# First weight splits, bias strips and the output projection's first weights, each at another place in a two-layer kernel

## The reference, cut to what matters

```python
def hybrid_layer(x, norm1_w, w_in, w_a2, b_a, gla_norm_w, w_out, norm2_w, w_ff1, w_ff2, rel_bias):
    h = rmsnorm(x, norm1_w)
    proj = h @ w_in
    aq, ak, av, bq, bk, bv, br, ba, cq, ck, cv = jnp.split(proj, ..., axis=-1)
    y_a = dilated_attention(heads(aq, 6), heads(ak, 6), heads(av, 6), bias_a)   # bias by distance
    y_b = gla(...)                                                              # gated linear attention
    y_c = moba_attention(heads(cq, 6), heads(ck, 6), heads(cv, 6), bias_c)      # bias by distance
    mix = jnp.concatenate([y_a, y_b, y_c], axis=-1)
    x = x + mix @ w_out
    h2 = rmsnorm(x, norm2_w)
    return x + jnp.square(jax.nn.relu(h2 @ w_ff1)) @ w_ff2
```

## Time and profile before

| what | us |
|---|---|
| median of three executions | 1555.93 (1555.65 to 1557.7) |
| profiled execution, its own time | 1553.91 |
| span of that execution, first to last instruction | 1552.1 |
| TensorE busy in the span | 1495.3 (96%) |
| ScalarE, VectorE, GpSimd busy | 577.2, 799.1, 657.9 |
| mean granted TensorE clock, of full speed | 0.987 |

### The profile page before, as it was taken

One profiled execution on the slowest core, in us unless ns is written; L12 is line 12 of the kernel. 1 busy time (PEld: TensorE's weight loads), 2 busy tenths in 40 slices (PEclk: granted clock), 3 DMA queues, 4 the chain that ended last, 5 costly groups with the idle time before them and its releaser, 6 DMA issues.

```text
span 1552.1 us, 21717 instructions
## 1 busy us (share of the span) xinstructions
PE 1495.3 (96%) x7323; PEld 1190.3 (77%) x7323; DVE 799.1 (51%) x1258; ACT 577.2 (37%) x948; POOL 657.9 (42%) x314
## 2 busy tenths in 40 slices
PE   8999999999999999999999899998999999999997
PEld 6778667788888888877768687665887888888886
DVE  4382384552443435864994505564556565654121
ACT  5412572431323223323972325553223232222222
POOL 4433455445444444434334345452443444444442
PEclk9999999999999999999999999999999999999998
DMA  5534202354555555423333234110332333333332
GB/s 154 157 88 117 82 28 69 124 178 153 174 158 158 168 163 168 129 68 94 91 81 90 60 103 75 35 41 14 95 95 68 99 100 99 95 95 91 98 94 85
DMA packets 285177, 160.27 MB, mean 103 GB/s; under 512 B 44930, under 2 KB 272770, under 8 KB 285114
## 3 DMA queue, kind: packets, MB, share of 16 engines
q1 hardware_dynamic: 285114, 159.46, 35.7%
HBM read 156.78 MB, written 5.80 MB: 105 GB/s over the span
## 4 chain that ended last, share of the span: by engine, by line
PE 48%; issue 34%; POOL 11%; DVE 3%; ACT 3%; DMA 1%; POOLq 0%; ACTq 0%; SPq 0%; DVEq 0%
PE ps L1981 13%; PE ps L1983 13%; PE ps L1982 13%; POOL WL L654 11%; PE ps L2464 2%; PE ps L2217 1%; PE ps L2475 1%; PE ps L2488 1%; PE ps L2277 1%; PE ps L2291 1%; PE ps L2334 1%; ACT WH L768 0%; DVE UL L1662 0%; ACT LP L1204 0%; DVE actL L1607 0%
## 5 line engine op out<-in xcount | busy, mean ns | idle before, releaser
L654 POOL TENSOR_TENSOR WL<-Wraw,WH 128x1024 fp32r<-128x1024 f32 (+2 forms) x239 | 573.2, 2399 | 810.3 <-ACT WH L768 810.3
L768 ACT ACTIVATE WH<-Wraw 128x1024 fp32r<-128x1024 f32 (+2 forms) x239 | 246.2, 1031 | 738.4 <-PE ps L1983 727.4
L1981 PE MATMUL ps<-actH,WH 128*128 128x512 f32 x1256 | 501.5, 399 | 15.7 <-POOL WL L654 8.8
L1983 PE MATMUL ps<-actH,WL 128*128 128x512 f32 x1256 | 490.5, 391 | 0.0
L1982 PE MATMUL ps<-actL,WH 128*128 128x512 f32 x1256 | 490.3, 390 | 0.0
L1981 PEld LDWEIGHTS ps<-actH,WH 128*128 128x128 f32 x1256 | 236.4, 188 | 82.2 <-issue 14.2
L1983 PEld LDWEIGHTS ps<-actH,WL 128*128 128x128 f32 x1256 | 236.5, 188 | 50.4
L1982 PEld LDWEIGHTS ps<-actL,WH 128*128 128x128 f32 x1256 | 236.6, 188 | 49.5 <-issue 2.9
L1981 PE MATMUL ps<-UH,WH 128*128 128x512 f32 x576 | 228.7, 397 | 7.8 <-DVE T L1835 4.1
L1983 PE MATMUL ps<-UH,WL 128*128 128x512 f32 x576 | 225.9, 392 | 0.0
L1982 PE MATMUL ps<-UL,WH 128*128 128x512 f32 x576 | 225.8, 392 | 0.0
(11 more groups left out here) (275 smaller groups left out, 1484.9 us busy)
## 6 DMA issues: line engine op xcount, KB each, us to landing
Wraw<-in_w_ff SPq DMA_DIRECT2D x64, 512.0 KB, 4.1
Wraw<-in_w_in SPq DMA_DIRECT2D x56, 512.0 KB, 3.9
wada<-in_w_ada SPq DMA_DIRECT2D x64, 384.0 KB, 4.5
Wraw<-in_w_up SPq DMA_DIRECT2D x44, 512.0 KB, 3.8
Wraw<-in_w_down SPq DMA_DIRECT2D x16, 448.0 KB, 3.7
Wraw<-in_w_proj_rnn SPq DMA_DIRECT2D x16, 320.0 KB, 3.1
Wraw<-in_w_proj_mla SPq DMA_DIRECT2D x8, 512.0 KB, 3.8
Wraw<-in_w_out SPq DMA_DIRECT2D x8, 512.0 KB, 3.8
```

What stands on the lines that cost most here:

```text
L654: nc.gpsimd.tensor_tensor(WL[slot][:, 0:kts, :], Wraw[slot][:, 0:kts, :], WH[slot][:, 0:kts, :].bitcast(F32), ALU.subtract).then_inc(s_lo, 1)
L768: A(WH[slot][:, 0:kts, :], Wraw[slot][:, 0:kts, :], ACT.Copy).then_inc(s_hi, 1)
L1981: MM(o, wh, ah, start=first, stop=False)
L1983: return MM(o, wl, ah, start=False, stop=last)
```

## The change

1. In the head ScalarE first loads its table with an activation on one column of `ones`, then splits weight block 0, then makes high parts 0 and 1, splits block 1, and goes on; the squares of x's first half are cut into two and two, and those of its last two quarters stand behind the last high parts. `x_squared` counts one more.
2. The strips' DMA leaves SyncE's queue and is issued by ScalarE, behind the `Silu` that ends the decay chain and ahead of the split of block 2 of `gQK`. The wait for the table stood there already.
3. The first two blocks of `gOut` are split behind `a_step(2)` and `a_step(3)`, on ScalarE and on GpSimd.
4. VectorE does `a_step(6)` ahead of `gla_low`; TensorE's first pair of `gOut` goes through the tiles as 0 to 4, 6, 7, 5 where it was 6, 7, 0 to 5.
5. The turning of the linear attention's result comes behind tile 6 of block 13, where it was behind tile 4.
6. The second norm's last sum comes at step 7, where it was at step 6.

```diff
@@ SyncE
             for c in range(4 * PAIRS // 2):
-                if c == 2:
-                    sp.wait_ge(S("tab_stored"), 16)
-                    sp.dma_start(strip_dram, bass.AP(tab_dram.tensor, P - 1, [[TAB, 2 * PAIRS], [-1, P], [1, SEQ]])
-                                 ).then_inc(S("strips_stored"), 16)
                 qk_load(c, c // 4, c % 4)
@@ GpSimd
                 for i in range(TB):
                     a_normalize(p, i)
-            lows(gOut, 2, 1)
+                if p in (2, 3):
+                    low(gOut.n0 + p - 2, gOut.slot(p - 2))
@@ ScalarE, head
+            act.wait_ge(S("ones_set"), 1)
+            A(T[5][:, 0:1], ones[:, 0:1], ACT.Copy).then_inc(S("x_squared"), 1)
+            highs(gB, 1, 1)
             act.wait_ge(S("vecs_turned"), 1)
             x_high(0)
             x_high(1)
-            highs(gB, 1, 1)
+            highs(gB, 1, 1, first=1)
             x_high(2)
             x_high(3)
             act.wait_ge(S("x_loaded0"), 16)
             act.wait_ge(S("x_loaded1"), 16)
-            x_squares(0, 2, 0, 2 * part)
-            highs(gB, 1, 1, first=1)
+            x_squares(1, 2, 0, 2 * part, range(2))
             x_high(4)
             x_high(5)
-            act.wait_ge(S("x_loaded2"), 16)
-            x_squares(TB, 3, 2 * part, 3 * part)
+            x_squares(3, 2, 0, 2 * part, range(2, TB))
             x_high(6)
             x_high(7)
+            act.wait_ge(S("x_loaded2"), 16)
+            x_squares(1 + TB, 3, 2 * part, 3 * part)
@@ ScalarE, behind the decay chain
             act.wait_ge(S("tab_stored"), 16)
+            nc.scalar.dma_start(strip_dram, bass.AP(tab_dram.tensor, P - 1, [[TAB, 2 * PAIRS], [-1, P], [1, SEQ]])
+                                ).then_inc(S("strips_stored"), 16)
@@ ScalarE, attention steps
             for p in range(1, PAIRS):
                 a_step(p)
-            highs(gOut, 2, 1)
+                if p in (2, 3):
+                    high(gOut, p - 2, gOut.n0 + p - 2, landed(gOut, p - 2))
@@ VectorE
-            for p in range(1, PAIRS):
+            for p in range(1, PAIRS + 1):
                 a_step(p)
             gla_low(0)
             gla_low(1)
-            a_step(PAIRS)
@@ TensorE
-                    if n == 13 and k == 4:
+                    if n == 13 and k == 6:
                         gla_turn_tokens()
...
-                         lambda j: free(gOut.b0 + j), [*range(PAIRS, KT), *range(PAIRS)])
+                         lambda j: free(gOut.b0 + j), [*range(PAIRS - 1), *range(PAIRS, KT), PAIRS - 1])
...
-                if step == 6:
+                if step == 7:
                     sum_last("n2")
```

More of the change, by code:

```diff
@@ L815, in x_high, with x_squares @@
                   ).then_inc(S("norm_high"), 1)
-            def x_squares(n0, at, a, b):
-                for t in range(TB):
-                    if n0 + t >= 6:
-                        act.wait_ge(S("x_squared"), n0 + t - 5)
-                    A(T[(n0 + t) % 6][:, 0:b - a], xn[:, t, a:b], ACT.Square, accum_out=rtok[:, at, t:t + 1]
+            def x_squares(n0, at, a, b, ts=range(TB)):
+                for n, t in enumerate(ts, n0):
+                    if n >= 5:
+                        act.wait_ge(S("x_squared"), n - 4)
+                    A(T[n % 5][:, 0:b - a], xn[:, t, a:b], ACT.Square, accum_out=rtok[:, at, t:t + 1]
                       ).then_inc(S("x_squared"), 1)
             part = D_MODEL // X_PARTS
+            act.wait_ge(S("ones_set"), 1)
+            A(T[5][:, 0:1], ones[:, 0:1], ACT.Copy).then_inc(S("x_squared"), 1)
+            highs(gB, 1, 1)
             act.wait_ge(S("vecs_turned"), 1)
@@ L833, in _ @@
             act.wait_ge(S("x_loaded1"), 16)
-            x_squares(0, 2, 0, 2 * part)
-            highs(gB, 1, 1, first=1)
+            x_squares(1, 2, 0, 2 * part, range(2))
             x_high(4)
             x_high(5)
-            act.wait_ge(S("x_loaded2"), 16)
-            x_squares(TB, 3, 2 * part, 3 * part)
+            x_squares(3, 2, 0, 2 * part, range(2, TB))
             x_high(6)
             x_high(7)
+            act.wait_ge(S("x_loaded2"), 16)
+            x_squares(1 + TB, 3, 2 * part, 3 * part)
             act.wait_ge(S("x_loaded3"), 16)
-            x_squares(2 * TB, 5, 3 * part, D_MODEL)
+            x_squares(1 + 2 * TB, 5, 3 * part, D_MODEL)
             act.wait_ge(S("const_loaded"), 16)
@@ L1350, in mean @@
                 if name == "n1":
-                    dve.wait_ge(S("x_squared"), 3 * TB)
+                    dve.wait_ge(S("x_squared"), 1 + 3 * TB)
                     own.done(V.tensor_tensor(rtok[:, 4, :], rtok[:, 2, :], rtok[:, 3, :], ALU.add))
```

## The result

Median 1547.46 us (1546.36 to 1550.23, 5 runs), where the kernel before has 1555.74 in the same series (1554.28 to 1557.7, 5 runs): ratio 0.9942, 95% interval 0.9929 to 0.9956, so 6.8 to 11.0 us less; the middle of that, 8.9, lies a little above the difference of the medians, 8.3. The forecast was 1551.5. The time is in the range (1547.0 to 1556.0) and the sign is right, but the gain is about twice the forecast's 4.4. The profiled execution took 1547.28, its span is 1545.5, where the kernel before had 1553.91 and 1552.1: 6.6 less.

The account below looks back on a forecast made before the run. TensorE, busy 1495.3 of 1552.1 us, bounds the kernel. -2.9 + 5.3 - 1.4 - 3.6 - 0.6 = -3.2 takes 1553.91 to 1550.7; the timed runs give 1551.0 to 1552.7, forecast 1551.5, range 1547.0 to 1556.0.

Parts of the forecast that it names:

- Head: Start of the kernel: ScalarE splits weight block 0 when it lands, TensorE starts sooner; 2.9 us gained, between 1.9 and 3.6.
- clock given back: Head: up to half of the half-clock stretch from 13.15 to 15.9 comes back, at most 1.1 us gained.
- Strips: Strips' DMA moved to ScalarE's queue, around block 2 of gQK: three losses, 5.3 us in sum, between 0 and 9.9.
- (a): Issue of the strips' DMA in ScalarE's queue ahead of block 2's split: 0.9 us lost, bounds 0 and 1.8.
- (b): Load of block 4 of gQK lands after 10.1 us where it has 7.4: 2.7 us lost.
- (c): Gap ahead of block 2 of gQK grows from 2.99 to 3.9, half clock follows: 1.7 us lost, bounds 0 and 3.4.
- Turning: Linear attention's turning, two tiles later, no longer waits for VectorE's oTok: 1.36 us gained, 1.4 in the sum.
- Steps and projection: Attention steps and output projection: 4.9 us gained at the end, 1.3 lost in steps 3 and 4, net 3.6 gained.
- Second norm: Second norm's last sum, one step later, loses most of its 0.96 us wait: 0.6 us gained.
- the strips are hidden: Rival: the load of block 4 of gQK lands within 7.4 us, giving 1548.0; chance 0.15.
- steps eaten: Rival: GpSimd's rests hold VectorE 2.4 us in two steps, or the clock stays low at the end; 1554.0, chance 0.25.
- strips starving SyncE's loads: Rival: blocks 4 and 5 of gQK each come 4.7 us late, 13.7 lost for 5.3; 1559.9, chance 0.05.

Follow-up runs that it names:

- head_alone: The kernel before with only ScalarE's new order at the head; ratio 0.9981 to the kernel before.
- strips_alone: The kernel before with only the strips' transfer moved to ScalarE's queue; ratio 1.0010 to the kernel before.
- strips_twice: The changed kernel with the strips' transfer issued a second time behind the first, into a tensor nobody reads; one time, 1555.43 us.
- turn_sum_alone: The kernel before with only the linear attention's turning two tiles later and the second norm's sum one step later; ratio 0.9982 to the kernel before.
- strips_pieces: The changed kernel with the strips' transfer in six pieces of two strips on SyncE's queue; ratio 1.0064 to the kernel before.
- gap_filled: The changed kernel with 20 idle matmuls in the 2.99 us gap ahead of block 2 of gQK; ratio 0.9945 to the kernel before.

## Where the prediction held and where it failed

**Head, -2.9.** Held: -2.8 by stretch A, -3.0 by the timed runs. Nearly all of it is the earlier start of the first product, 2.6 on the mean of these kernels; of the two smaller terms, clock given back and a late copy on VectorE, neither was measured by itself. The profile that was to show the clock back from about 13 on had it back at 15.1; in head_alone it was back at 13.6. A single comparison with the profile before would have said -2.0.

**Strips, +5.3.** This is the step that failed, and the most of the error: +0.4 by the means of stretch B, +0.9 without the half clock at 30, +1.6 (between -0.3 and 3.6) by strips_alone, +2.0 where the profile before had no half clock. Of its terms:
- (a), 0.9 for the issue: nothing. I put it in series with the split, though the DMA instruction had 3.5 us of ScalarE's own work to lie under, from 66.2 to 69.7. With two transfers it did delay the split, by 1.6.
- (b), 2.7 for a landing of 10.1: it was 9.3, and 1.9 to 2.0 were lost. The mechanism was right, the size a little high. One reason shows in the trace: the transfer was issued at 66.2, not 73, and 1.43 of its 3.15 MB were gone when the load was issued. By the rule that the Trainium skill gives in DMA: Bandwidth & Descriptors, section Queues, rings and completion order, each DMA engine goes round its queues a packet at a time. The trace agrees where both queues are full (1154 packets and 1151, in strips_twice). The landings don't test it as well: 0.5 MB with four times as many bytes of strips are 2.5 MB, 8.6 us at 0.29 MB a us, and what a usual load takes beyond its bytes (3.9 less 1.7) makes 10.8, an estimate from these rows. Measured were 9.3 and, beside two transfers, 12.1; why the second is above it stays open.
- (c), 1.7 for the half clock behind the gap: I took it as an addition caused by a longer gap. The gap of 2.99 as it was brings it, in the kernels with the old place as well (76.50, 76.48 and 75.17 in stretch B, each with 1.7 of half clock at 30 besides), and in the changed one it lies within the wait for block 4. Late load and half clock are two lower bounds for the same start, and the larger counts, not the sum. This accounts for all ten values of B within 0.3: 71.96, with 1.7 where half clock stands at 30, and the larger of 2.0 for a late load and what half clock costs behind the gap (0, 1.7 or 3.1). That is why the move costs 2.0 against a profile without that half clock and next to nothing against those with it.

**Turning, -1.4.** Held: -1.1 by stretch C, in which turn_sum_alone has a chance half clock of 1.7 at 149; -1.4 without that kernel.

**Steps and projection, -3.6.** -2.8 by stretch D, so the term was mis-sized by 0.8, and by 0.3 without the half clock at D's start. Its halves were both off. The divisions take 1.28 each, but a step lengthens only from 8.76 to 8.93, by 0.17 for the 0.65 priced: held for 1.0, VectorE has 0.61 of idle time to give in the step, and where the other 0.2 went isn't traced. The end gives about 3.1, not 4.9, since 4.9 counts a half clock that one of four profiles had. Without half clock on either side, D is 49.90 and 47.19. Half clock at the start of D, behind the wait of 1.41, is no part of the change: it stands in two of four profiles as before and in four of six with the new order.

**Second norm, -0.6.** -1.7 by stretch E. The wait that goes is as forecast; missed was that half clock follows it in three of four profiles. The profile before was the one that was spared.

**Sum.** -3.2 forecast, -8.0 by the stretches. Of the 4.8 between them, the strips are 4.9 and the second norm 1.1; the other way go the steps with 0.8, the turning with 0.3 and the head with 0.1. Without the half clock at untouched places it is 5.1: strips 4.4 and second norm 1.1, less 0.3 for the steps and 0.1 for the head. The forecast of the time took off another 1.2, because the medians might already hold term (c)'s half clock; three of the five profiles with the strips as before do hold it. That guess was sound, and it stood beside a sum that counted the same half clock as new.

**Rivals.** The first, that the strips are hidden, came nearest (1548.0, given 0.15), but not by its mechanism: the load wasn't in time. The others, steps eaten and strips starving SyncE's loads, didn't come; strips_pieces is what such starving looks like, for another reason. The base was the deeper fault: the prediction read the half clock of one execution as the kernel's, and counted it as sure where it stood (end of the steps) and as absent where it didn't (block 2, second norm).

## What to carry to other kernels

Where a gap of TensorE is followed by half clock in one profile and not in the next, price it at its mean over several profiles, and price a change by stretches between fixed places rather than by the whole time. Two delays that end in the same start don't add; before an addition, ask which of them would be waited for if the other were gone. And a gap that can't be closed can be filled: idle matmuls that end just inside it kept the clock in each gap tried, and in four gaps they brought 8 us once the strips no longer delayed a load. Too many of them run past the gap, by 1.2 in gap_filled.

## What the runs showed of the hardware

- Half clock (1.2 for 2.4 GHz) comes behind a gap in one profile and not in another: behind 2.99 us ahead of block 2 it stood in 7 of the 9 profiles of the table above without a fill there, behind 0.97 in 3 of 4, behind 2.37 at the end of the steps in 1 of 4, behind 2.94 to 3.01 at 802 to 814 in all ten. Each time it cost 1.6 to 3.1 us. What decides it is not shown, and no kernel was profiled twice; that the executions of one kernel differ likewise is seen from their mean clock (0.981 to 0.990).
- How many DMA engines a transfer used went by its outermost dimension. A piece with 2 outermost moved at 48 GB/s with a DMA share of 0.14; the whole transfer, with 12, had this window to itself in the changed kernel:

```profile
70.00:73.00 3.00, 0.24 (x2) 0.00 (x0) 2.72 (x4) 3.00 (x5) 2.18 (x1) 1.00 0.76 275
```

  The Trainium skill, DMA: Bandwidth & Descriptors, section Rules for kernel authors, states that an outermost dimension smaller than 16 confines the transfer to at most as many engines. The trace agrees: 2 of 16 are 0.125 for the 0.14 measured, 12 of 16 are 0.75 for 0.76. The issuing queue stood still with the slow pieces, 4.8 to 5.3 us for 0.5 MB, where a piece with 12 outermost was issued in 0.75 us and held up no load.
- A DMA instruction in ScalarE's queue went out while earlier operations of ScalarE were still to run (at 66.18, with a table load and three operations to come), and held the next operation only where it lasted longer than these: 1.33 us long it cost nothing, a second one of 3.76 behind it cost 1.6.
- While both queues were full, the strips' and the loads' queues moved packet for packet, 1154 and 1151 from 84 to 94 in strips_twice.
